# Turning rows by quarters of the PE array in two expert stages, and recurrent scores by halves of 64 keys

## The chip, the cores and the metric

One core of one Trainium2 chip runs the whole program. The time is that of the device in microseconds, from the first to the last instruction and what lies around them; the median of three executions is compared. A core has five engines with a queue of instructions each: TensorE (PE; its weight loads are listed as PEld), VectorE (DVE), ScalarE (ACT), GpSimd (POOL) and SyncE (SP, which here only starts transfers). Matmuls write to PSUM, and DVE or ACT copy the result to SBUF. A matmul has a stationary operand, whose columns are loaded into the array first, and a moving operand, which streams through.

## The reference

Two transformer blocks on 1024 tokens of width 1024, all in float32. The first has a recurrent branch, attention and a mixture of 32 experts, two per token. The second has a gated linear recurrence (HGRN2) beside a pooling branch and a mixture of 64 experts, eight per token. What the change touches:

```python
def block_ffn(args):                  # for each block of tokens of one expert
    xb, e = args
    return (jax.nn.silu(xb @ w_gate[e]) * (xb @ w_up[e])) @ w_down[e]
...
def step(state, inp):                 # HGRN2, per head, chunk by chunk
    ...
    decay = jnp.where(causal, jnp.exp(jnp.minimum(diff, 0.0)), 0.0)
    scores = jnp.einsum('bhtk,bhsk,bhtsk->bhts', qb, kb, decay)
    o_intra = jnp.einsum('bhts,bhsv->bhtv', scores, vb)
```

## The kernel before

The program runs stage after stage, each a set of instruction queues written by hand, one per engine, joined by semaphores. PE executes its queue in order.

**Experts** (`experts`, called once with 32 and once with 64 experts). A step works on two half blocks of 64 tokens, which may belong to two experts. Half A uses columns 0 to 63 of the array and the expert's weights `w_gu`/`w_dn`; half B uses columns 64 to 127 and a staged copy (`st_gu`, `st_dn`, in the tiles `h` or `second`). PE's order in step i is: eight pairs of gate/up matmuls into `gu_ps` (L1870 and L1873, 512 columns each, one pair per chunk of 128 of the 1024 inputs); the turns of the next step's token rows (`turn_rows`, L1859: eight transposes of 128x128 into `x_ps`); the down matmuls of step i-1 into `y_ps` (L1896, L1899, in `finish`); the turns of this step's activation (L1882, two transposes into `h_ps`). Token rows arrive in `moe_xb` by an indirect gather that POOL starts one step and more ahead. DVE copies `x_ps` to `x_t` (L1947) and `h_ps` to `hid_t` (L1949), multiplies the activation (L1945), and stages half B's weights (L1940, L1933). Before the down matmuls PE's sequencer reads the block's expert number from memory (L1887) and works out addresses (L1896); L1857, 1740 and 1864 do the like elsewhere.

**Recurrence** (`hgrn`, four heads). For each tile t of 128 tokens, `scores` (L2120) forms eight 128x128 products, one per level of a halving of the tile and one for the diagonal, into one half of the PSUM tile `big`. DVE multiplies all 8x128 columns by `mask` (L2274) and adds them up over the levels (L2287) into `sc`. PE then multiplies `sc` by the values (L2154) and the carried state by the queries (L2157). Between the scores of tile t+1 and these products PE runs a part of the next head's projection (L2101), except in the last head.

Of the kernel before, what the change touches and what calls it, by code (L numbers as in the profile page):

```python
# [21 lines left out]
ALU = mybir.AluOpType  # L22
ACT = mybir.ActivationFunctionType
AX = mybir.AxisListType.X

P = 128
S = 1024
D = 1024
T = S // P
C = D // P  # L30
BANK = 512
# [13 lines left out]
PART = P // 2  # L45
# [1650 lines left out]


def experts(nc, G, E, NB, W, rows_d, sum_d, loaded, stage, work):

# [3 lines left out]
    ph = phase(nc)  # L1703
    FC = F_EXP // P
    with ph.ctx:
# [5 lines left out]
        xb, idx, mark = G.xb, G.idx, G.mark  # L1711
        act_g = ph.sb("act_g", [P, 2, F_EXP])
        hid = ph.sb("hid", [P, 2, F_EXP])
        hid_t = ph.sb("hid_t", [P, 2, FC, P])
# [6 lines left out]
        y = work[:, 4 * D:6 * D].rearrange("p (s n) -> p s n", s=2)  # L1721
        x_ps = ph.ps("x_ps", [P, C, P])
        gu_ps = ph.ps("gu_ps", [P, 2, 2, F_EXP])
        h_ps = ph.ps("h_ps", [P, BANK // P, P])[:, 0:FC, :]
        y_ps = ph.ps("y_ps", [P, D])
# [129 lines left out]
        def _(pe):  # L1855
            def turn_rows(b, slot, landed):
                pe.wait_ge(x_in[slot], landed)  # L1857
                for c in range(C):
                    last = nc.tensor.transpose(x_ps[:, c, :], xb[:, slot, c:D:C], G.ident[:])  # L1859
                last.then_inc(x_turned, 1)  # L1860

            def step(i, slot, rounds):
# [18 lines left out]
                for c in range(FC):  # L1881
                    last = nc.tensor.transpose(h_ps[:, c, :], hid[:, slot, c::FC], G.ident[:])  # L1882
                last.then_inc(h_turned, 1)
# [41 lines left out]
        def _(v):  # L1925
            d = nc.vector
# [16 lines left out]
            def step(i, slot, rounds):  # L1943
                v.wait_ge(silu_done, i + 1)
                d.tensor_tensor(hid[:, slot, :], act_g[:, slot, :], gu_ps[:, slot, 1, :], ALU.mult).then_inc(hid_ready, 1)  # L1945
                v.wait_ge(x_turned, i + 2)
                d.tensor_copy(x_t[:, 1 - slot], x_ps[:]).then_inc(x_ready, 1)  # L1947
                v.wait_ge(h_turned, i + 1)
                d.tensor_copy(hid_t[:, slot], h_ps).then_inc(h_ready, 1)  # L1949
                v.wait_ge(share_in, i + 1)  # L1950
                d.tensor_copy(share[PART:P, slot:slot + 1], share_b[PART:P, slot:slot + 1]).then_inc(share_ready, 1)
                stage_down(i)
                stage_gate_up(i + 2, slot)

            stage_gate_up(0, 0)
            v.wait_ge(x_turned, 1)
            d.tensor_copy(x_t[:, 0], x_ps[:]).then_inc(x_ready, 1)  # L1957
            stage_gate_up(1, 1)
# [22 lines left out]
def hgrn(nc, A, G):  # L1981
# [8 lines left out]
    ph = phase(nc)  # L1990
# [11 lines left out]
    with ph.ctx:  # L2002
# [17 lines left out]
        kd_t = ph.sb("kd_t", [P, T, P])  # L2020
        sm = ph.sb("sm", [P, N, P])
        sc = ph.sb("sc", [P, 2, P])
# [7 lines left out]
         sc_ps, sc_taken, sc_ready, kt_ready, kt_taken, o_ready, o_taken, u_ready, st_ready, root_in,  # L2030
         rooted, o_done, turned, turn_taken, lb_ready) = ph.sems(
            "w0 w1 w2 w3 gain_in masked proj proj_taken dve act to_exp exped kd_ready lev_ready "
            "sc_ps sc_taken sc_ready kt_ready kt_taken o_ready o_taken u_ready st_ready root_in "
            "rooted o_done turned turn_taken lb_ready")
        w_in_sem = [w0, w1, w2, w3]
# [45 lines left out]
        def _(pe):  # L2081
# [30 lines left out]
            def scores(h, t):  # L2112
                cs = slice(t * P, (t + 1) * P)
                if t == 0:
                    pe.wait_ge(proj_taken, 1 + h * 4 + 4)
                else:
                    pe.wait_ge(sc_taken, h * T + t)
                for lev in range(N):
                    kk, qq = (qk[:, lev, cs], qk[:, lev, cs]) if lev < LEVELS else (k[:, cs], q[:, cs])
                    last = nc.tensor.matmul(big[:, 1, lev * P:(lev + 1) * P], kk, qq, start=True, stop=True)  # L2120
                last.then_inc(sc_ps, 1)

            def head(h, more):
# [24 lines left out]
                for t in range(T):  # L2148
                    if t + 1 < T:
                        scores(h, t + 1)  # L2150
                        if more:
                            project(h + 1, 0, [t + 1])
                    pe.wait_ge(sc_ready, h * T + (t + 1))
                    last = nc.tensor.matmul(ko_ps[:, t, :], sc[:, t % 2, :], val[:, t, :], start=True, stop=t == 0)  # L2154
# [58 lines left out]
        def _(v):  # L2213
# [8 lines left out]
            v.wait_ge(lb_ready, 2)  # L2222
            v.wait_ge(masked, MASKED)
            v.wait_ge(gain_in, 16)

# [5 lines left out]
            with v.Fori(0, H) as h:  # L2231
# [38 lines left out]
                for t in range(T):  # L2270
                    v.wait_ge(sc_ps, h * T + (t + 1))
                    if t:
                        v.wait_ge(sc_ready, h * T + t)
                    d.tensor_tensor(sm[:].rearrange("p n t -> p (n t)"), big[:, 1],  # L2274
                                    mask[:].rearrange("p n t -> p (n t)"), ALU.mult).then_inc(sc_taken, 1)
                    if t == 0:
# [7 lines left out]
                    v.wait_ge(sc_taken, h * T + (t + 1))  # L2284
                    if t >= 2:
                        v.wait_ge(o_ready, h * T + (t - 1))
                    d.tensor_reduce(sc[:, t % 2, :], sm[:].rearrange("p n t -> p t n"), AX, ALU.add).then_inc(sc_ready, 1)  # L2287

# [488 lines left out]
```

## Time and profile before

| | |
|---|---|
| three executions | 3523.74, 3524.87, 3526.46 us, median 3524.87 |
| profiled execution | 3527.6 us, its span 3525.9 us |
| mean granted PE clock | 0.952 of 2.4 GHz |
| PE busy | 91% of the span |
| DVE, ACT, POOL busy | 45%, 21%, 20% |
| DMA | 564.82 MB, mean 160 GB/s |

The trace records each instruction with its start. The ends of matmuls are modelled, so differences between starts are what counts. A plain float32 matmul appears as two records with a weight load each, a transpose as one. The end of a wait is put down to what released it; "issue" means that the engine waited for nothing that the profile shows.

### The profile page before, as it was taken

Reading aid. Unit: us, or ns where it says so; the run is one execution under the profiler, and the core shown is the slowest. Engines: PE = TensorE matmul, PEld = TensorE weight load, DVE = VectorE, ACT = ScalarE, POOL = GpSimd, SP = SyncE. Lnnn points to the kernel's source line nnn. Section 1 sums busy time; section 2 is a strip of 40 time slices with the busy share of each in tenths; the row PEclk is TensorE's granted clock in tenths of the full one; section 3 lists DMA queues with packets and bytes.
Section 4 is the critical chain, followed back from the end, with each engine's and each line's share of the span. In section 5 each row is a group of like instructions: output and inputs, shape, how many; then the busy total and the mean of one; then the engine's idle time right before and its main releaser. Section 6 shows DMA issues by size and latency. Waiting matters only on the chain. (4 is left out here: it accounts for less than half of the span.)

```text
span 3525.9 us, 44548 instructions
## 1 busy us (share of the span) xinstructions
PE 3216.6 (91%) x14147; PEld 1603.9 (45%) x14148; DVE 1579.0 (45%) x2360; ACT 728.2 (21%) x1169; POOL 714.7 (20%) x919
## 2 busy tenths in 40 slices
PE   8999999978999995989789997989899999999992
PEld 4444445545665454333267773455333333333330
DVE  3322224456774123434347773334444444444444
ACT  2221223334552001111023330121011111111112
POOL 1000000000000000344400000000355555555552
PEclk9999999998999996999889998989999999999996
DMA  6210021123221215899531001211788998988876
GB/s 225 96 42 30 0 102 53 49 62 79 73 72 60 73 66 217 316 386 383 181 129 36 24 1 75 75 76 56 270 276 274 351 327 297 309 282 280 272 248 185
DMA packets 177205, 564.82 MB, mean 160 GB/s; under 512 B 18636, under 2 KB 88880, under 8 KB 139952
## 3 DMA queue, kind: packets, MB, share of 16 engines
q1 hardware_dynamic: 139456, 428.64, 32.1%
q0 software_dynamic: 34416, 128.50, 14.9%
q10 hardware_dynamic: 3240, 6.45, 0.5%
q8 instruction: 58, 0.95, 0.1%
q14 instruction: 35, 0.29, 0.0%
HBM read 460.27 MB, written 103.27 MB: 160 GB/s over the span
## 5 line engine op out<-in xcount | busy, mean ns | idle before, releaser
L1870 PE MATMUL gu_ps<-w_gu,second 128*64 x1680 | 754.8, 603 | 12.9 <-DVE second L1957 7.8
L1873 PE MATMUL gu_ps<-h,second 128*64 128x512 f32 x1680 | 754.8, 603 | 0.0
L1870 PEld LDWEIGHTS gu_ps<-w_gu,second 128*64 128x64 f32 x1680 | 224.2, 138 | 455.2 <-issue 443.3
L1503 POOL COPY moe_idx<-moe_slot_tok 128x1 int32<-128x1 int32 x4 | 0.6, 185 | 1878.1 <-DVEq L1438 1236.5
L1896 PE MATMUL y_ps<-w_dn,hid_t 128*64 x824 | 375.6, 598 | 0.2
L1899 PE MATMUL y_ps<-second,hid_t 128*64 128x512 f32 x824 | 375.6, 598 | 0.0
L355 PE MATMUL front<-second,wcol 128*128 128x512 f32 x768 | 332.1, 595 | 4.9 <-ACTq L63 2.5
L1933 DVE COPY h<-w_gu 128x4096 f32 x109 | 249.4, 2288 | 93.4 <-SPq L1751 88.4
L355 PEld LDWEIGHTS front<-second,wcol 128*128 128x128 f32 x768 | 146.3, 191 | 189.8 <-issue 189.8
L1819 POOL TENSOR_TENSOR idx_y<-moe_slot_tok,moe_side 128x1 int32<-128x1 int32 x103 | 122.7, 1191 | 522.5 <-ACT second L1919 522.5
L1873 PEld LDWEIGHTS gu_ps<-h,second 128*64 128x64 f32 x1680 | 224.1, 138 | 0.0
L1919 ACT ACTIVATE second<-y_ps,share 128x1024 f32<-128x1024 f32 x103 | 114.7, 1114 | 456.4 <-PE y_ps L1899 456.4
L1913 ACT ACTIVATE act_g<-gu_ps 128x256 f32<-128x256 f32 x105 | 40.3, 384 | 734.3 <-PE gu_ps L1873 734.3
L1896 PEld LDWEIGHTS y_ps<-w_dn,hid_t 128*64 128x64 f32 x824 | 104.3, 136 | 189.2 <-issue 177.3
L1823 POOL TENSOR_TENSOR mark_y<-tok 128x1 f32<-128x1 f32 x103 | 180.2, 1750 | 20.6 <-DMA token_sums<-second,idx_y 9.9
L1824 POOL DMA_INDIRECT token_sums<-second,idx_y x103 | 176.0, 1708 | 18.3 <-issue 17.4
L1945 DVE TENSOR_TENSOR hid<-act_g,gu_ps 128x256 f32<-128x256 f32 x105 | 44.1, 420 | 291.1 <-ACT act_g L1913 291.0
L1949 DVE COPY hid_t<-h_ps 128x256 f32<-128x256 f32 x105 | 44.5, 424 | 275.8 <-PE h_ps L1882 275.8
L1859 PEld LDWEIGHTS x_ps<-ident,moe_xb 128*128 128x128 f32 x856 | 104.4, 193 | 105.0 <-issue 94.3
L1940 DVE COPY second<-w_dn 128x2048 f32 x105 | 128.9, 1228 | 47.2 <-issue 46.2
L1859 PE MATMUL x_ps<-ident,moe_xb 128*128 128x128 f32 x856 | 125.1, 290 | 18.7 <-PEq L95 17.9
L1947 DVE COPY second<-x_ps 128x1024 f32<-128x1024 f32 x105 | 128.5, 1224 | 24.3 <-PE x_ps L1859 24.3
(449 smaller groups left out, 4904.6 us busy)
## 6 DMA issues: line engine op xcount, KB each, us to landing
w_gu<-in_w_gate_dram SPq DMA_DIRECT2D x96, 1024.0 KB, 12.8
w_gu<-in_w_up_dram SPq DMA_DIRECT2D x96, 1024.0 KB, 15.8
w_dn<-in_w_down_dram SPq DMA_DIRECT2D x96, 1024.0 KB, 10.7
wcol<-in_w_in_dram SPq DMA_DIRECT2D x12, 1024.0 KB, 5.4
qk_by_head<-stage SPq DMA_DIRECT2D x32, 384.0 KB, 3.7
qk<-qk_by_head SPq DMA_DIRECT2D x16, 768.0 KB
token_sums<-zero POOLq DMA_DIRECT2D x19, 512.0 KB, 12.9
token_sums<-second SPq DMA_DIRECT2D x16, 512.0 KB, 2.6
```

The lines of the kernel that those rows point to most:

```text
L355: last = nc.tensor.matmul(ps[:, slot, c, h * BANK:(h + 1) * BANK], wcol[:, k, kc, c * P:(c + 1) * P], G.u[:, kc, h * BANK:(h + 1) * BANK], ...
L1819: g.tensor_tensor(idx_y[:, slot:slot + 1], G.slot_tok[:, bass.ds(b, 1)], G.side, ALU.add).then_inc(idx_y_ready, 1)
L1823: g.tensor_tensor(mark_y[:, slot:slot + 1], G.tok[:, 0:1], G.tok[:, 0:1], ALU.add).then_inc(idx_y_ready, 1)
L1824: g.indirect_dma_start(sum_d, bass.IndirectOffsetOnAxis(ap=idx_y[:, slot:slot + 1], axis=0), y[:, slot, :], None, compute_op=ALU.add).then ...
L1859: last = nc.tensor.transpose(x_ps[:, c, :], xb[:, slot, c:D:C], G.ident[:])
L1870: nc.tensor.matmul(gu_ps[0:PART, slot], x_t[:, slot, c, 0:PART], w_gu[:, bass.ds(ws, 1), :, c, :].rearrange("p o g n -> p (o g) n"), start ...
L1873: last = nc.tensor.matmul(gu_ps[PART:P, slot], x_t[:, slot, c, PART:P], st_gu[:, slot, :, c, :], start=c == 0, stop=c == C - 1)
L1896: nc.tensor.matmul(y_ps[0:PART, cs], hid_t[:, slot, c, 0:PART], w_dn[:, bass.ds(ws, 1), c, cs].rearrange("p o n -> p (o n)"), start=c == 0 ...
L1899: last = nc.tensor.matmul(y_ps[PART:P, cs], hid_t[:, slot, c, PART:P], st_dn[:, c, cs], start=c == 0, stop=c == FC - 1)
L1933: d.tensor_copy(st_gu[:, slot].rearrange("p g c n -> p (g c n)"), w_gu[:, bass.ds(e % W, 1)].rearrange("p o g c n -> p (o g c n)")).then_i ...
L1940: d.tensor_copy(st_dn.rearrange("p c n -> p (c n)"), w_dn[:, bass.ds(e % W, 1)].rearrange("p o c n -> p (o c n)")).then_inc(d_staged, 1)
L1947: d.tensor_copy(x_t[:, 1 - slot], x_ps[:]).then_inc(x_ready, 1)
```

## The change

The transposes of the experts are replaced by plain matmuls with the identity. For the first chunk (`whole`) the full 128x128 block is loaded twice, and 64 columns of the identity are streamed each time. Each further chunk is cut into four quarters of 64x64, each on its own tile of the array, with row half a of the source going to PSUM bank a. `x_ps` and `h_ps` are laid out as two banks for this, and the copies read them in the matching order. In the recurrence the tile of scores is formed only where it is needed: seven products (six levels and the diagonal) for keys and queries of the same half, on two column halves, and one 64x64 product for the widest level. They go to alternate halves of `big[:, 1]`, so `scores` of tile 1 no longer waits for the mask of tile 0. DVE copies the wide piece, masks 448 instead of 1024 columns, and reduces in two instructions of 64 partitions.

```diff
+def turn_quarters(nc, G, out, src, whole):
+    for a in range(2):
+        rows = slice(a * PART, (a + 1) * PART)
+        if whole:
+            last = nc.tensor.matmul(out[:, a, :], src, G.ident[:, rows], start=True, stop=True)
+            continue
+        for b in range(2):
+            cols = slice(b * PART, (b + 1) * PART)
+            last = nc.tensor.matmul(out[cols, a, :], src[rows, cols], G.ident[rows, rows], start=True, stop=True)
+    return last
...
-        x_ps = ph.ps("x_ps", [P, C, P])
+        x_ps = ph.ps("x_ps", [P, 2, C, PART])
-        h_ps = ph.ps("h_ps", [P, BANK // P, P])[:, 0:FC, :]
+        h_ps = ph.ps("h_ps", [P, 2, BANK])[:, :, 0:FC * PART].rearrange("p a (c n) -> p a c n", c=FC)
...
-                    last = nc.tensor.transpose(x_ps[:, c, :], xb[:, slot, c:D:C], G.ident[:])
+                    last = turn_quarters(nc, G, x_ps[:, :, c, :], xb[:, slot, c:D:C], c == 0)
...
-                    last = nc.tensor.transpose(h_ps[:, c, :], hid[:, slot, c::FC], G.ident[:])
+                    last = turn_quarters(nc, G, h_ps[:, :, c, :], hid[:, slot, c::FC], c == 0)
...
-                d.tensor_copy(x_t[:, 1 - slot], x_ps[:]).then_inc(x_ready, 1)
+                d.tensor_copy(x_t[:, 1 - slot].rearrange("p c (a n) -> p a c n", a=2), x_ps[:]).then_inc(x_ready, 1)
...
-        sm = ph.sb("sm", [P, N, P])
+        mask_h = ph.sb("mask_h", [P, LEVELS, PART])
+        sm = ph.sb("sm", [P, LEVELS, PART])
...
-                if t == 0:
+                if t < 2:
                     pe.wait_ge(proj_taken, 1 + h * 4 + 4)
                 else:
-                    pe.wait_ge(sc_taken, h * T + t)
-                for lev in range(N):
+                    pe.wait_ge(sc_taken, h * T + (t - 1))
+                to = t % 2 * BANK
+                for n, lev in enumerate([*range(LEVELS - 1), LEVELS]):
                     kk, qq = (qk[:, lev, cs], qk[:, lev, cs]) if lev < LEVELS else (k[:, cs], q[:, cs])
-                    last = nc.tensor.matmul(big[:, 1, lev * P:(lev + 1) * P], kk, qq, start=True, stop=True)
-                last.then_inc(sc_ps, 1)
+                    for half in range(2):
+                        hs = slice(half * PART, (half + 1) * PART)
+                        nc.tensor.matmul(big[hs, 1, to + n * PART:to + (n + 1) * PART], kk[:, hs], qq[:, hs],
+                                         start=True, stop=True)
+                wide = qk[:, LEVELS - 1, cs]
+                nc.tensor.matmul(big[0:PART, 1, to + LEVELS * PART:to + N * PART], wide[:, 0:PART], wide[:, PART:P],
+                                 start=True, stop=True).then_inc(sc_ps, 1)
...
+                    pe.wait_ge(wide_taken, h * T + (t + 1))
+                    pe.wait_ge(low_ready, h * T + (t + 1))
                     pe.wait_ge(sc_ready, h * T + (t + 1))
...
+            hv = Steps(v, halved)
+            for half in range(2):
+                hs = slice(half * PART, (half + 1) * PART)
+                hv(d.tensor_copy(mask_h[hs, 0:LEVELS - 1], mask[hs, 0:LEVELS - 1, hs]))
+                hv(d.tensor_copy(mask_h[hs, LEVELS - 1], mask[hs, LEVELS, hs]))
+            hv(d.memset(sc[PART:P, :, 0:PART], 0.0))
...
-                    d.tensor_tensor(sm[:].rearrange("p n t -> p (n t)"), big[:, 1],
-                                    mask[:].rearrange("p n t -> p (n t)"), ALU.mult).then_inc(sc_taken, 1)
+                    d.tensor_copy(sc[0:PART, t % 2, PART:P], big[0:PART, 1, to + LEVELS * PART:to + N * PART]
+                                  ).then_inc(wide_taken, 1)
+                    d.tensor_tensor(sm[:].rearrange("p n t -> p (n t)"), big[:, 1, to:to + LEVELS * PART],
+                                    mask_h[:].rearrange("p n t -> p (n t)"), ALU.mult).then_inc(sc_taken, 1)
...
-                    d.tensor_reduce(sc[:, t % 2, :], sm[:].rearrange("p n t -> p t n"), AX, ALU.add).then_inc(sc_ready, 1)
+                    d.tensor_reduce(sc[0:PART, t % 2, 0:PART], sm[0:PART].rearrange("p n t -> p t n"), AX,
+                                    ALU.add).then_inc(low_ready, 1)
+                    d.tensor_reduce(sc[PART:P, t % 2, PART:P], sm[PART:P].rearrange("p n t -> p t n"), AX,
+                                    ALU.add).then_inc(sc_ready, 1)
```

In PE's queue of an expert step, from the last gate/up matmul to the first down matmuls, there stood before (each name is output<-inputs, and the last numbers are partitions x columns of the output):

```order
L1873 MATMUL gu_ps<-h,second 64x512
L1859 MATMUL x_ps<-ident,moe_xb 128x128 x8
L1887 TENSOR_LOAD moe_blk_e
L1887 ISA x2
L1888 REGISTER_ALU
L1896 ISA
L1896 MATMUL y_ps<-w_dn,hid_t 64x512
L1899 MATMUL y_ps<-second,hid_t 64x512
```

and in the changed kernel at the same place (TENSOR_LOAD and what follows it is the sequencer's preparation of the down matmuls):

```order
L1886 MATMUL gu_ps<-h,second 64x512
L1703 MATMUL x_ps<-ident,moe_xb 128x64 x2
L1707 MATMUL x_ps<-ident,moe_xb 64x64 x28
L1900 TENSOR_LOAD moe_blk_e
L1900 ISA x2
L1901 REGISTER_ALU
L1909 ISA
L1909 MATMUL y_ps<-w_dn,hid_t 64x512
```

Thirty matmuls stand where eight transposes stood; nothing else has moved. In PE's queue of the recurrent stage, a head's second and third scores stood before as

```order
L2120 MATMUL big<-qk 128x128 x7
L2120 MATMUL big<-q,k 128x128
L2101 MATMUL big<-h,w 128x512 x2
L2154 MATMUL ko_ps<-val,sc 128x128
L2117 REGISTER_ALU
L2120 MATMUL big<-qk 128x128 x7
```

and in the changed kernel, around the same projection part (L2101 before, L2115 now), as

```order
L2139 MATMUL big<-qk 64x64 x12
L2139 MATMUL big<-q,k 64x64 x2
L2142 MATMUL big<-qk 64x64
L2115 MATMUL big<-h,w 128x512 x2
L2175 ISA
L2178 MATMUL ko_ps<-val,sc 128x128
L2139 MATMUL big<-qk 64x64 x12
```

Eight matmuls of a tile have become fifteen of a quarter of the area each, in the same place of the queue.

## Rows read from the trace of the kernel before

**Rows 1.** Windows: length, busy PE, PEld, DVE, ACT, POOL, clock, DMA share, GB/s.

```profile
1411.52:1744.15 332.63, 310.12 (x1434) 115.23 (x1434) 138.96 (x147) 35.41 (x49) 141.81 (x190) 0.96 0.91 332
...
2491.41:3461.09 969.68, 968.12 (x4624) 363.16 (x4624) 449.67 (x477) 117.72 (x159) 517.40 (x627) 1.00 0.86 287
```

**Rows 2.** The same two expert stages, instructions on tile act_g alone (one activation a step).

```profile
1411.52:1744.15 332.63, 10.47 (x25) 9.61 (x25) 0.96 0.91 332
2491.41:3461.09 969.68, 33.67 (x80) 30.72 (x80) 1.00 0.86 287
```

**Rows 3.** Timeline of PE in one expert step: start, us, engine, line, operands.

```profile
3007.10 0.59 PE L1870 MATMUL gu_ps<-w_gu,second 128*64 x1
...
3007.63 1.15 PE L1859 MATMUL x_ps<-ident,moe_xb 128*128 128x128 f32 x8
3008.71 0.64 PE L1896 MATMUL y_ps<-w_dn,hid_t 128*64 x1
```

**Rows 4.** The same timeline, end of that step and start of the next.

```profile
3011.76 0.59 PE L1896 MATMUL y_ps<-w_dn,hid_t 128*64 x1
...
3012.30 0.50 PE L1882 MATMUL h_ps<-ident,hid 128*128 128x128 f32 x2
3012.73 0.64 PE L1870 MATMUL gu_ps<-w_gu,second 128*64 x1
```

**Rows 5.** Groups by line and shape: records, busy us, mean ns, idle before.

```profile
L1870 PE MATMUL gu_ps<-w_gu,second 128*64 x1680 | 754.8, 603 | 12.9 <-DVE second L1957 7.8 <-DVE second L1947 5.1
...
L1859 PE MATMUL x_ps<-ident,moe_xb 128*128 128x128 f32 x856 | 125.1, 290 | 18.7 <-PEq L95 17.9 <-DMA moe_xb<-token_rows,moe_idx 0.8
...
L2106 PE MATMUL big<-w,h 128*128 128x128 f32 x1024 | 115.0, 275 | 0.0
...
L1945 DVE TENSOR_TENSOR hid<-act_g,gu_ps 128x256 f32<-128x256 f32 x105 | 44.1, 420 | 291.1 <-ACT act_g L1913 291.0
```

**Rows 6.** Timeline of PE in the router's matmuls.

```profile
1289.86 1.87 PE L1162 MATMUL ps<-w_route,h 128*128 128x36 f32 x16
```

**Rows 7.** Timeline of PE and its weight loads (PEld) in one gate/up group.

```profile
3000.61 0.13 PEld L1870 LDWEIGHTS gu_ps<-w_gu,second 128*64 128x64 f32 x1
...
3000.61 0.13 PEld L1873 LDWEIGHTS gu_ps<-h,second 128*64 128x64 f32 x1
...
3000.66 0.14 PEld L1870 LDWEIGHTS gu_ps<-w_gu,second 128*64 128x64 f32 x1
...
3003.23 0.59 PE L1870 MATMUL gu_ps<-w_gu,second 128*64 x1
```

**Rows 8.** Timeline of a step whose token rows landed late.

```profile
2898.39 1.16 PE L1859 MATMUL x_ps<-ident,moe_xb 128*128 128x128 f32 x8 [0.28 <-DMA moe_xb<-token_rows,moe_idx]
...
2899.63 0.64 PE L1896 MATMUL y_ps<-w_dn,hid_t 128*64 x1
```

**Rows 9.** Line 1887 in that step; PEldq is PE's sequencer; first and last start.

```profile
L1887 PEldq FUSED_REGOPS  x2: 42/96/151, 2898.4 to 2898.9; - x2
```

**Rows 10.** Line 1857 in the step of rows 7.

```profile
L1857 PEldq FUSED_REGOPS  x1: 42/42/42, 3003.3 to 3003.3; - x1
```

**Rows 11.** Timeline of PE in the recurrent stage, one tile of a head.

```profile
2028.15 0.39 PE L2157 MATMUL ko_ps<-state,qb 128*128 128x128 f32 x2
2028.37 1.73 PE L2120 MATMUL big<-qk 128*128 128x128 f32 x14
...
2030.16 1.88 PE L2101 MATMUL big<-h,w 128*128 128x512 f32 x4
...
2032.10 0.28 PE L2157 MATMUL ko_ps<-state,qb 128*128 128x128 f32 x1
```

**Rows 12.** Timeline of DVE in the last head of that stage.

```profile
2104.73 1.94 DVE L2287 TENSOR_REDUCE sc<-sm 128x128 f32<-128x1024 f32 x1
2106.84 1.22 DVE L2274 TENSOR_TENSOR sm<-big,mask 128x1024 f32<-128x1024 f32 x1 [0.17 <-PE big L2120]
2108.09 1.93 DVE L2287 TENSOR_REDUCE sc<-sm 128x128 f32<-128x1024 f32 x1
```

More of the change, by code:

```diff
@@ L1946, in step @@
                 v.wait_ge(x_turned, i + 2)
-                d.tensor_copy(x_t[:, 1 - slot], x_ps[:]).then_inc(x_ready, 1)
+                d.tensor_copy(x_t[:, 1 - slot].rearrange("p c (a n) -> p a c n", a=2), x_ps[:]).then_inc(x_ready, 1)
                 v.wait_ge(h_turned, i + 1)
-                d.tensor_copy(hid_t[:, slot], h_ps).then_inc(h_ready, 1)
+                d.tensor_copy(hid_t[:, slot].rearrange("p c (a n) -> p a c n", a=2), h_ps).then_inc(h_ready, 1)
                 v.wait_ge(share_in, i + 1)
@@ L1956, in _ @@
             v.wait_ge(x_turned, 1)
-            d.tensor_copy(x_t[:, 0], x_ps[:]).then_inc(x_ready, 1)
+            d.tensor_copy(x_t[:, 0].rearrange("p c (a n) -> p a c n", a=2), x_ps[:]).then_inc(x_ready, 1)
             stage_gate_up(1, 1)
@@ L2030, in hgrn @@
          sc_ps, sc_taken, sc_ready, kt_ready, kt_taken, o_ready, o_taken, u_ready, st_ready, root_in,
-         rooted, o_done, turned, turn_taken, lb_ready) = ph.sems(
+         rooted, o_done, turned, turn_taken, lb_ready, wide_taken, low_ready, halved) = ph.sems(
             "w0 w1 w2 w3 gain_in masked proj proj_taken dve act to_exp exped kd_ready lev_ready "
             "sc_ps sc_taken sc_ready kt_ready kt_taken o_ready o_taken u_ready st_ready root_in "
-            "rooted o_done turned turn_taken lb_ready")
+            "rooted o_done turned turn_taken lb_ready wide_taken low_ready halved")
         w_in_sem = [w0, w1, w2, w3]
@@ L2223, in _ @@
             v.wait_ge(masked, MASKED)
+            hv = Steps(v, halved)
[4 more added lines that the diff above has]
+            hv(d.memset(sc[PART:P, :, 0:PART], 0.0))
+            hv.join()
             v.wait_ge(gain_in, 16)
@@ L2273, in _ @@
                         v.wait_ge(sc_ready, h * T + t)
-                    d.tensor_tensor(sm[:].rearrange("p n t -> p (n t)"), big[:, 1],
-                                    mask[:].rearrange("p n t -> p (n t)"), ALU.mult).then_inc(sc_taken, 1)
+                    if t >= 2:
+                        v.wait_ge(o_ready, h * T + (t - 1))
+                    to = t % 2 * BANK
+                    d.tensor_copy(sc[0:PART, t % 2, PART:P], big[0:PART, 1, to + LEVELS * PART:to + N * PART]
+                                  ).then_inc(wide_taken, 1)
+                    d.tensor_tensor(sm[:].rearrange("p n t -> p (n t)"), big[:, 1, to:to + LEVELS * PART],
+                                    mask_h[:].rearrange("p n t -> p (n t)"), ALU.mult).then_inc(sc_taken, 1)
                     if t == 0:
@@ L2284, in _ @@
                     v.wait_ge(sc_taken, h * T + (t + 1))
-                    if t >= 2:
-                        v.wait_ge(o_ready, h * T + (t - 1))
-                    d.tensor_reduce(sc[:, t % 2, :], sm[:].rearrange("p n t -> p t n"), AX, ALU.add).then_inc(sc_ready, 1)
+                    d.tensor_reduce(sc[0:PART, t % 2, 0:PART], sm[0:PART].rearrange("p n t -> p t n"), AX,
+                                    ALU.add).then_inc(low_ready, 1)
+                    d.tensor_reduce(sc[PART:P, t % 2, PART:P], sm[PART:P].rearrange("p n t -> p t n"), AX,
+                                    ALU.add).then_inc(sc_ready, 1)
                 v.wait_ge(proj_taken, 1 + h * 4 + 4)
```

## The prediction

> **What bounds the kernel now.** I read the page first: TensorE is busy for 91% of the span (in the table above). Such a share says little alone, so next come the windows of the stages that the change touches [rows 1, 2]. The reader is to see two things there. The second expert stage is 969.68 us long with PE busy for 968.12 us at a granted clock of 1.00, that is 2.4 GHz, and ran 80 steps (80 activations of act_g): 12.12 us a step. The first ran 25 steps in 332.63 us; at 12.13 us a step these are 303.3 us, so 29 us of it are waits for weights that had not landed (DMA share 0.91).
>
> Then the timeline of one expert step, PE alone [rows 3, 4]. Everything in it follows without a gap: the last gate/up pair starts at 3007.10, the eight turns of the rows (L1859) at 3007.63, the first down pair at 3008.71, the last at 3011.76, the two turns of the activation (L1882) at 3012.30, the next gate/up pair at 3012.73. So whatever the turns get longer or shorter by, the step gets longer or shorter by. A gate/up pair takes 0.43 us (3000.61 to 3003.23 are six of them, the first 0.48 [rows 7]).
>
> **What a turn costs now.** Eight turns span 1.15 us with the last record's own 0.275, so the last one starts 0.88 us after the first: 0.21 to the second, then 0.11 each [rows 3, 5]; the second is 0.1 late because its load, too, had to wait for the new shape. The two neighbours work on column halves (128*64), the turns on the whole array (128*128), and each change of shape shows: the last gate/up pair to the first turn is 0.53, 0.10 more than a pair; the last turn to the down pair 1.08 - 0.88 = 0.20, of which 0.11 is the turn; and the first pair after a change is 0.48 instead of 0.43, as the load of 64 columns is not hidden then. A change costs about 0.10 us plus a bare load: 0.05 for 64 columns, 0.10 for 128. The 0.11 of a turn is its load, not its columns: the router's matmuls, only 36 columns wide, start as far apart (sixteen records in 1.87 - 0.28 us, fifteen steps of 0.106), and those of L2106, 128 columns, take 115.0/1024 = 0.112 [rows 5, 6]. The load of 64 columns must then be about 0.055, and the two column halves load side by side (L1870 and L1873 both at 3000.61, the next of L1870 at 3000.66) [rows 7].
>
> **What replaces it.** A turn is one record (856 for 107 blocks); a plain f32 matmul is two (L1870: 8 matmuls a step, 1680 records in 105 steps), each with its own load [rows 5]. Per block of rows the change puts 2 whole matmuls (4 records, 128 columns loaded) and 28 quarter ones (56 records) for 8. A quarter record loads 64 columns, 0.055, beside the one before it, and streams 64 columns; 512 take 0.43, so 64 take 0.054. If the four tiles run side by side as the two column halves do, a group of four records takes 0.056: 14 groups. From the first start: whole records at 0, 0.21, 0.32 and 0.44; change of shape, first group at 0.64; second at 0.75 (bare load); last at 0.75 + 12 x 0.056 = 1.42; down pair at 1.42 + 0.15 = 1.57. Against 1.08 that is +0.49 us. For the activation: 0.44 + 0.20 = 0.64, second group 0.75, next gate/up pair 0.90, against 0.43: +0.47. The quarters cannot win even so, since the seven quartered chunks stream 7 x 2 x 0.056 = 0.78 where seven turns took 0.77, and two more changes of shape and the doubled first chunk come on top.
>
> **Who issues them.** The sequencer works in order. After the turns it fetches the block's expert for the down matmuls (L1887 on), and how long that takes is seen where rows came late: turns start at 2898.39, L1887 begins at 2898.4 (all eight turns were then issued), the down pair starts at 2899.63 [rows 8, 9]. So 1.2 us from the last turn issued to the down pair, now hidden because the issue runs ahead. How far ahead: L1857, behind all gate/up matmuls, runs at 3003.3, when the seventh of sixteen pairs has just started: 18 matmul records outstanding [rows 7, 10]. With sixteen records of turns they all fit. With 60 the last is issued when 18 are left, 4.5 groups or 0.25 us before the last start: at 1.17. Then 1.2 us: down pair at 2.37 against 1.08. **+1.29 us instead of +0.49.** Behind the activation's turns (12 records) the same kind of preparation for gate/up has the 3.5 us of down matmuls as cover; if that cover were gone it would cost up to 0.5 us more. The next gather of rows is issued off a longer step, so it is not late.
>
> The Trainium skill (TensorE: Matmul & The Clock Gate, first table) gives the TensorE queue as 64 instructions deep. Rows 7 and 10 show 18 matmul records, 34 with their loads. By a depth of 64 the preparation would begin 0.2 us earlier, the step would grow by 1.56, and the sum would be some 20 us lower.
>
> So a step grows by 1.29 + 0.47 = 1.76 us. Second stage: 80 x 1.76 = +141. First stage: 25 x 1.76 = 44, less what the 29 us of waiting for weights take up; the waits come in three places and the loads themselves wait for freed slots, so I take about 20 as absorbed: +24 (bounds +15 and +44). The first blocks' turns: +1. The copies out of PSUM keep their elements, and DVE is busy for less than half of this stage [rows 1]. The larger program is left at nothing: PE's other instructions do not change.
>
> **Recurrent scores.** Per tile of 128 tokens PE now runs sixteen records of 0.112 from 2028.37, then four of the next projection from 2030.16, and with two small products comes round in 3.95 us (2028.15 to 2032.10 for the second product) [rows 11]. After: 28 records in pairs on two column halves, 14 x 0.056, two more for the wide piece, 0.11, and two changes of shape. From the product's last start to the projection's second: 0.20 + 0.11 + 12 x 0.056 + 0.11 + 0.15 + 0.54 = 1.78, against 17 x 0.112 + 0.43 = 2.33: -0.55 us. Three heads x 8: -13. The second scores of each head no longer wait for the first mask: -0.6 x 3. In the last head there is no projection and DVE sets the pace: 2104.73 to 2108.09, 3.36 us for a reduction of 1.94 and a mask of 1.22 [rows 12]. After: copy 0.22 (estimate from 0.42 for 256 elements [rows 5]), mask 448/1024 elements 0.62, two reductions of 0.85 to 0.92 each (half the partitions, 448 elements): about 2.75, -0.6 x 8 = -5. In the other heads 2.75 stays below PE's new 3.4, so that cover holds; if it did not, the gain would end at 3.95 - 2.75 = 1.2. Copies that build mask_h fall before the first head's activation and are left at nothing; without cover, +2. Sum -20 (bounds -12 and -28).
>
> **Sum:** 141 + 24 + 1 - 20 = +146 on the profiled execution's 3527.6 us, 3673.6. That execution is 2.7 above the median 3524.87, so 3671.
>
> **Rivals.**
> The four tiles do not load or start side by side in full: no row of this kernel shows row halves. If the two row halves load one after another, a group takes 0.11: the last starts at 0.64 + 0.165 + 12 x 0.11 = 2.13, issued 0.5 earlier, down pair at 2.83, +1.75; activation +0.53. Step +2.28: 182 + 37 + 1 - 20 = 200, 3725. Chance 0.20. The Trainium skill (the same page, "Wait — 56ns, not 53.3ns?") says that starts of matmuls never come closer than about 25 ns on average however small they are. By it a group of four would take 0.1 and the time would be near 3713. Two loads start together in rows 7, but no row has four matmuls within 0.056 us, so the trace neither bears it out nor excludes it.
>
> The records of one matmul and the next stay in order and do not overlap across tiles: 0.056 a record, the last start at 0.75 + 54 x 0.056 = 3.77, issued 1.0 earlier, down pair at 3.97, +2.9; activation +0.8. 80 x 3.7 + 92 - 20 + 1 - 20 = 349: 3874. Against it: column halves pair in every step [rows 7]. 0.12.
>
> The preparation stays hidden (a deeper queue, or records of quarters that count for less): step +0.96, 77 + 10 (of 24, the rest absorbed) + 1 - 20: 3593. Against it: rows 7 and 10. 0.12.
>
> PE's clock falls to 1.2 GHz in part of the step, since it now idles for 0.8 us: a tenth of the step at half speed is +1.2 us, +126 on top: about 3800. Against it: the clock is still 0.96 in the first stage with its 29 us of waits [rows 1]. 0.04.
>
> Faster: the changes of shape are free when the matmuls around them are tiled too, and a quarter record costs 0.03. Then the turns take 0.45 + 14 x 0.03 = 0.87 for 1.08 and 0.45 + 2 x 0.03 = 0.51 for 0.43, and two bare loads of 0.05 go: about 0.2 us off each step: 105 x 0.2 + 20 gives 3484. It decides where a step grows by less than 20/105 = 0.19 us. Against it: a change between 128*64 and 128*128 costs in each step [rows 3, 4]. 0.05, no change at all 0.02. What is left, 0.45, is my forecast, alone from 3640 to 3710.
>
> **Range.** From 3585 (the hidden preparation) to 3790 (row halves that load in turn, nothing absorbed in the first stage, +20, and the cover of the gate/up preparation gone, 80 x 0.5 = +40): 0.77 and a little of the clock's case. This kernel's runs lie within 0.1%, so 0.2% (7 us) is about what can be told from no change. Slower 0.93, within 0.02, faster 0.05.
>
> **What would show it.** Periods of the gate/up pairs near 13.9 us in the second stage; 60 records per block in the turns, groups of four starts 0.056 apart; PE idle of about 0.8 us before each down pair, put down to issue; fewer weight waits in the first stage; recurrent stage 20 us shorter with scores of 1.2 us. Wrong would be: groups at 0.1 or more, no idle before the down pair, or a step below 12.3 us.

## The result and the profile after

The changed kernel takes 3776.09 us (median, 3771.84 to 3778.22) against 3525.27 for the kernel before (3523.74 to 3526.46) beside it: 7.2% longer, ratio 1.0715, 95% interval 1.0698 to 1.0732. The forecast was 3671 with a range of 3585 to 3790. So the sign and the range held, but the loss is 251 us where 146 were forecast. Its profiled span is 3770.2 us, 244 above the 3525.9 of before.

The windows of the two expert stages (columns as in [rows 1]):

```profile
1409.84:1785.80 375.96, 366.92 (x2984) 172.59 (x2984) 139.64 (x147) 35.77 (x49) 125.60 (x190) 0.98 0.84 294
2508.67:3707.70 1199.03, 1171.43 (x9584) 551.74 (x9584) 449.75 (x477) 118.10 (x159) 408.35 (x627) 0.99 0.74 232
```

Against [rows 1] the first stage grew by 43.3 us (forecast 24) and the second by 229.4 (forecast 141). What lies outside the two got 28 us shorter (244.3 - 272.7), where 19 were forecast. So the surplus over the forecast sits in the expert steps. This is PE's timeline of one step, to be laid beside [rows 3, 4]:

```profile
3024.53 0.59 PE L1883 MATMUL gu_ps<-w_gu,second 128*64 x1
...
3025.05 1.16 PE L1703 MATMUL x_ps<-ident,moe_xb 128*128 128x64 f32 x4
3026.15 1.91 PE L1707 MATMUL x_ps<-ident,moe_xb 64*64 64x64 f32 x56
3028.39 0.64 PE L1909 MATMUL y_ps<-w_dn,hid_t 128*64 x1 [0.33 <-issue]
...
3031.97 0.68 PE L1703 MATMUL h_ps<-ident,hid 128*128 128x64 f32 x4
3032.58 0.35 PE L1707 MATMUL h_ps<-ident,hid 64*64 64x64 f32 x8
3032.86 0.64 PE L1883 MATMUL gu_ps<-w_gu,second 128*64 x1
```

Read it in differences of starts. From the first turn to the first down pair it is 3.34 us, where it was 1.08 and 2.37 were forecast. From the activation's turns to the next gate/up pair it is 0.89, where it was 0.43 and 0.90 were forecast. The step is 14.84 us instead of 12.12 (forecast 13.88). So all of the surplus, 0.96 us, lies between the first turn of the token rows and the first down pair. Two parts of that stretch are longer than forecast: four whole records take 1.10 us to the first quarter (forecast 0.64), and the fourteen groups of four take 1.91 - 0.285 (the last record's own) = 1.63 us (forecast 0.78). Part of this is given back ahead of the down pair (below). The groups by form of the loads (PEld), and of the down matmuls, say more:

```profile
L1707 PEld LDWEIGHTS x_ps<-ident,moe_xb 64*64 64x64 f32 x5992 | 190.0, 212 | 7.3
L1703 PEld LDWEIGHTS x_ps<-ident,moe_xb 128*128 128x128 f32 x428 | 109.7, 329 | 103.8 <-issue 103.8
L1703 PEld LDWEIGHTS h_ps<-ident,hid 128*128 128x128 f32 x420 | 57.5, 196 | 83.7 <-issue 83.6
L1707 PEld LDWEIGHTS h_ps<-ident,hid 64*64 64x64 f32 x840 | 22.4, 134 | 7.1
```

```profile
L1909 PE MATMUL y_ps<-w_dn,hid_t 128*64 x824 | 392.1, 621 | 35.2 <-issue 35.2
```

The same helper loads the same shapes for `x_ps` in 329 and 212 ns and for `h_ps` in 196 and 134. What differs is the source: `moe_xb` is read with a step of 8 elements (`c:D:C`), `hid` with a step of 2 (`c::FC`). And there is the idle time ahead of the down matmuls put down to issue that was forecast, 0.33 us in the step above (forecast some 0.8). Line 1900, which reads the expert's number, ran in that step at (PEldq is PE's sequencer; last numbers are first and last start)

```profile
L1900 PEldq FUSED_REGOPS  x2: 42/96/151, 3027.2 to 3027.6; - x2
```

that is 0.6 us before the last turn starts (3026.15 + 1.63 = 3027.78) and 1.2 us before the down pair.

**Ten long steps.** Ten of the 105 steps take 16.55 us instead of 14.84. Windows of one ordinary step and of the long one behind it:

```profile
3602.07:3616.91 14.84, 14.50 (x126) 6.87 (x121) 5.65 (x6) 1.50 (x3) 5.17 (x8) 1.00 0.88 282
3616.91:3633.44 16.53, 16.20 (x126) 7.28 (x121) 5.65 (x6) 1.50 (x3) 5.23 (x8) 0.90 0.52 143
```

and PE's timeline inside the second:

```profile
3627.26 0.91 PE L1909 MATMUL y_ps<-w_dn,hid_t 128*64 x1 [0.33 <-issue]
...
3628.82 1.06 PE L1909 MATMUL y_ps<-w_dn,hid_t 128*64 x1
...
3629.67 1.06 PE L1909 MATMUL y_ps<-w_dn,hid_t 128*64 x1
```

The down pairs behind the turns stand 0.85 us apart instead of 0.43: twice as long, the lower level of 1.2 GHz, and the granted clock of the step is 0.90 for 1.00. That costs 10 x 1.7 = 17 us in all. The hit steps do not lie at random: the seven of the second stage start at 2627.0, 2777.2, 2927.3, 3122.0, 3272.1, 3466.8 and 3616.9, that is 10 or 13 steps apart (150.1 to 150.2 or 194.7 us), and nothing in between.

**The recurrent stage.** PE's timeline of one tile (beside [rows 11]) and DVE's in the last head (beside [rows 12]):

```profile
2064.93 0.39 PE L2181 MATMUL ko_ps<-state,qb 128*128 128x128 f32 x2
2065.25 0.92 PE L2139 MATMUL big<-qk 128*64 128x64 f32 x24
...
2066.33 1.98 PE L2115 MATMUL big<-h,w 128*128 128x512 f32 x4
...
2068.37 0.39 PE L2181 MATMUL ko_ps<-state,qb 128*128 128x128 f32 x2
```

```profile
2121.81 0.22 DVE L2308 COPY sc<-big 64x64 f32<-64x64 f32 x1
2122.05 0.62 DVE L2310 TENSOR_TENSOR sm<-big,mask_h 128x448 f32<-128x448 f32 x1
2122.71 0.93 DVE L2321 TENSOR_REDUCE sc<-sm 64x64 f32<-64x448 f32 x1
2123.67 0.91 DVE L2323 TENSOR_REDUCE sc<-sm 64x64 f32<-64x448 f32 x1
2124.68 0.22 DVE L2308 COPY sc<-big 64x64 f32<-64x64 f32 x1
```

A tile comes round in 3.44 us where it was 3.95 (forecast 3.40), and in the last head DVE's cycle is 2.87 where it was 3.36 (forecast 2.75). From the first product with the state (L2157, now L2181) to the last the stage takes 240.15 us where it took 259.59.

### The profile page after: what moved, and what is told of

Read it like the earlier page. It is cut to its first block and busy times, and to the rows that moved or that the text cites. A ratio compares the mean times of both kernels' runs of the same rounds, so it can differ in the third digit from the quotient of the medians.

```text
span 3770.2 us, 58750 instructions
## 1 busy us (share of the span) xinstructions
PE 3454.8 (92%) x21209; PEld 1825.2 (48%) x21210; DVE 1566.1 (42%) x2429; ACT 727.8 (19%) x1169; POOL 586.4 (16%) x919
## 3 DMA queue, kind: packets, MB, share of 16 engines
q8 instruction: 66, 1.08, 0.1%
## 5 line engine op out<-in xcount | busy, mean ns | idle before, releaser
L1909 PE MATMUL y_ps<-w_dn,hid_t 128*64 x824 | 392.1, 621 | 35.2 <-issue 35.2
L1912 PE MATMUL y_ps<-second,hid_t 128*64 128x512 f32 x824 | 392.6, 621 | 0.0
L1837 POOL DMA_INDIRECT token_sums<-second,idx_y x103 | 324.1, 3146 | 45.7 <-issue 45.6
L1707 PE MATMUL x_ps<-ident,moe_xb 64*64 64x64 f32 x5992 | 204.8, 285 | 0.0
L1707 PEld LDWEIGHTS x_ps<-ident,moe_xb 64*64 64x64 f32 x5992 | 190.0, 212 | 7.3
L1832 POOL TENSOR_TENSOR idx_y<-moe_slot_tok,moe_side 128x1 int32<-128x1 int32 x103 | 19.1, 186 | 894.5 <-ACT second L1932 894.5
```

What stands on the lines that cost most here:

```text
L1707: last = nc.tensor.matmul(out[cols, a, :], src[rows, cols], G.ident[rows, rows], start=True, stop=True)
L1837: g.indirect_dma_start(sum_d, bass.IndirectOffsetOnAxis(ap=idx_y[:, slot:slot + 1], axis=0), y[:, slot, :], None, compute_op=ALU.add).then ...
L1909: nc.tensor.matmul(y_ps[0:PART, cs], hid_t[:, slot, c, 0:PART], w_dn[:, bass.ds(ws, 1), c, cs].rearrange("p o n -> p (o n)"), start=c == 0 ...
L1912: last = nc.tensor.matmul(y_ps[PART:P, cs], hid_t[:, slot, c, PART:P], st_dn[:, c, cs], start=c == 0, stop=c == FC - 1)
```

## Experiments

Theories of the surplus: (A) a plain float32 matmul loads a source whose elements lie 32 bytes apart in twice the time, and the four tiles do run side by side; (B) the tiles of the two row halves load in turn (a rival of the prediction); (C) two starts cannot come closer than some floor, whatever is loaded. And of the wait before the down pair: the sequencer's preparation is exposed, or it is not. The kernels below that turn other elements of the rows route the second block's tokens otherwise and run a step or two more, so steps are compared, not only totals. A kernel for which no interval is given was executed once, and its steps are read from that profile.

**The two parts apart.** `scores_only` has the experts of before and the recurrent stage of the change; `experts_only` the other way round.

> The experts as before (eight transposes a step), the recurrent scores as changed. Theory A, the two parts of the change are independent and the recurrent stage alone gained its 22 us: 3525.3 - 22 = 3503 us (ratio 0.9938), both expert stages as long as before (332.6 and 969.7 us within 1). Rival, the gain of the recurrent stage is given back behind it, where weights or rows wait on something else: 3518 or more. What would show it is the sum of the expert stages being some 15 us longer.

> The recurrent scores as before, the experts as changed. If the parts are independent: 3776 + 22 = 3798 us, expert steps of 14.84 us in the second stage as in the changed kernel, and again about ten steps of 105 that are 1.7 us longer with down matmuls at a lower clock. Rival: the longer steps depend on the rest of the program, and they are fewer or at other places: 3780.

Measured: `scores_only` 3506.09 us, ratio 0.9938 (0.9916 to 0.9961). Its windows of the experts, 24 steps and 78 steps from start to start,

```profile
1408.70:1729.02 320.32, 298.36 (x1376) 110.77 (x1376) 133.31 (x141) 33.92 (x47) 137.06 (x182) 0.95 0.93 342
2469.67:3415.96 946.29, 944.96 (x4508) 354.44 (x4509) 438.52 (x465) 114.80 (x155) 494.52 (x611) 1.00 0.88 291
```

are as long as before (320.50 and 945.52 for the same steps), so nothing is given back. `experts_only` took 3800.21 us; its usual step is 14.84 us, and eleven are about 1.7 us longer (forecast some ten), at other places. The parts are independent: 3506 + 3800 - 3527 (before, beside them) = 3779 for the 3776 of the changed kernel.

**Neighbouring elements.** `unit_stride` is the changed kernel with

```diff
-  last = turn_quarters(nc, G, x_ps[:, :, c, :], xb[:, slot, c:D:C], c == 0)
+  last = turn_quarters(nc, G, x_ps[:, :, c, :], xb[:, slot, c * P:(c + 1) * P], c == 0)
```

> The changed kernel with one edit: the turns of the token rows read 128 neighbouring elements of a row instead of every eighth one, so the chunks hold other inputs than the weights expect; the instructions, their number and their tiles stay. Theory A, the load of a source with a step of 8 elements (32 bytes) takes twice as long as that of a source without, and the four tiles load side by side: whole records 0.112 us apart instead of 0.237, groups of four 0.056 instead of 0.120, last turn 1.4 us after the first instead of 2.74, and the wait for the preparation shows in full (1.17 + 1.2 = 2.4 us from the first turn to the first down pair, where it was 3.35): step 14.84 - 0.95 = 13.9 us, the whole 3776 - 105 x 0.95 = 3676 us. Rival B, the tiles of the two row halves load in turn, whatever the source: groups stay 0.12 apart and only the first four whole records come closer, by 0.4 us in all: step 14.4 us, 3734. Rival C, a floor of starts: groups at 0.10, step about 14.5.

Measured: 3693.12 us with 107 steps instead of 105, most of them 13.91 us long, and none with its down matmuls at the lower clock. PE's timeline, the load group by form, and line 1900:

```profile
2979.33 0.66 PE L1703 MATMUL x_ps<-ident,moe_xb 128*128 128x64 f32 x4
2979.92 1.04 PE L1707 MATMUL x_ps<-ident,moe_xb 64*64 64x64 f32 x56
...
2981.74 0.64 PE L1909 MATMUL y_ps<-w_dn,hid_t 128*64 x1 [0.78 <-issue]
```

```profile
L1707 PEld LDWEIGHTS x_ps<-ident,moe_xb 64*64 64x64 f32 x6104 | 101.2, 136 | 8.5 <-issue 0.8
```

```profile
L1900 PEldq FUSED_REGOPS  x2: 42/96/151, 2980.5 to 2981.0; - x2
```

The load fell from 212 to 136 ns, the quarters span 1.04 - 0.22 (own) = 0.82 us for 14 groups, the last turn starts 1.41 us after the first and the down pair at 2.41. These are the prediction's 1.42 and 2.37, though two misses of about 0.05 us cancel in the first: the quarters begin at 0.59 (forecast 0.64) and span 0.82 (forecast 0.78). Rival B (groups of 0.12) and rival C (0.10) are out. The preparation begins 0.21 us before the last turn starts, with 16 records of turns still to start (forecast 0.25 and 18), and the wait put down to issue is 0.78, as forecast; in the changed kernel itself the slower turns covered 0.60 us of the preparation.

**How the price depends on the step.** `stride4` reads every fourth element (`xb[:, slot, c * PART:c * PART + BANK:4]`), `stride2` every second.

> The changed kernel with the turns of the token rows reading every fourth element (16 bytes) instead of every eighth (32 bytes), other inputs again. It tells how the load grows with the step: if it doubles only beyond 16 bytes, groups of four are 0.056 apart and the step is 13.9 us as with neighbouring elements; if it grows evenly, 1.5 times (0.085, step about 14.2); if any step costs double, 0.120 and 14.84. The activation's turns, whose step is 2 elements, went at 0.118 for 128 columns, which speaks against the last. I take 13.9, 3680 to 3695 us.

> The changed kernel with the turns of the token rows reading every second element (8 bytes), other inputs again. A step of 16 bytes cost as much as one of 32, and the activation's turns, with a step of 8 bytes, loaded in 0.118 us for 128 columns. If that low price belongs to the step: whole records 0.118 apart, groups of four 0.06, last turn 1.45 us after the first, step 13.9, whole 3695 us (with the two more blocks of the other unit-order kernels). If instead anything but neighbours costs double and the activation was spared for another reason (its tile, its few records): groups 0.120 and step 14.84, 3795.

The groups by form of the loads, first `stride4`, then `stride2`:

```profile
L1707 PEld LDWEIGHTS x_ps<-ident,moe_xb 64*64 64x64 f32 x6104 | 192.9, 211 | 7.5
```

```profile
L1707 PEld LDWEIGHTS x_ps<-ident,moe_xb 64*64 64x64 f32 x6048 | 103.2, 137 | 8.2 <-issue 0.7
```

`stride4` took 3795.74 us with steps of 14.81 us, and my 13.9 for it was wrong: 16 bytes cost all that 32 cost. `stride2` took 3678.43 us with steps of 13.96, 0.05 above those of neighbours. Over the four steps tried (1, 2, 4 and 8 elements) the price is a jump between 8 and 16 bytes, not a slope; a step of three was not run. The Trainium skill (SBUF — State Buffer, under Door 1: The DMA port swizzle) has SBUF read in lines of 16 bytes, at full speed only where at least two accesses fall on one line. Two float32 elements that lie 8 bytes apart can share such a line and two that lie 16 apart cannot, and the trace agrees (137 ns at two, 211 at four); the page's own figure of four float32 for free is not what these runs show. I had not looked at it for the prediction. The rule would have warned that these loads cost more; how much more it does not say.

**A plain whole matmul, and a transpose.** `plain_whole` is the kernel before with its eight transposes written as plain matmuls, and `transpose_unit` the kernel before with transposes of neighbours:

```diff
-  last = nc.tensor.transpose(x_ps[:, c, :], xb[:, slot, c:D:C], G.ident[:])
+  last = nc.tensor.matmul(x_ps[:, c, :], xb[:, slot, c:D:C], G.ident[:], start=True, stop=True)
```

> The kernel before, its eight transposes of the token rows written as eight plain 128x128 matmuls with the identity (16 records, whole array, same source with a step of 8 elements); nothing is in quarters. Theory A, a plain float32 matmul loads a source of that step in 0.237 us for 128 columns: sixteen records span 15 x 0.237 + 0.05 = 3.6 us from first to last, the preparation behind them is hidden (16 records fit in what runs ahead), so the first down pair stands 3.9 us after the first turn, a step is 12.12 + 2.8 = 14.9 us, the whole some 3525 + 105 x 2.8 = 3820 us less a little weight waiting. Rival B, the slow loads belong to quarters and to what mixes with them: 15 x 0.112 + 0.1 = 1.8 us, step 13.0, whole 3620.

> The kernel before with its eight transposes reading 128 neighbouring elements of a row, so the chunks hold other inputs than the weights expect. Theory A, a transpose (one record) isn't slowed by the step of its source, as its 0.11 us was already that of loads without a step: turns 0.11 apart as before, step 12.12, whole 3525 us but for a block or two more or fewer of the second routing. Rival B, transposes pay for the step too and would go at 0.056: step 12.12 - 0.4 = 11.7, whole 3483 us.

Timeline of PE and the load group of `plain_whole`:

```profile
3048.59 4.07 PE L1859 MATMUL x_ps<-ident,moe_xb 128*128 128x128 f32 x16
3052.59 0.64 PE L1896 MATMUL y_ps<-w_dn,hid_t 128*64 x1
```

```profile
L1859 PEld LDWEIGHTS x_ps<-ident,moe_xb 128*128 128x128 f32 x1712 | 415.4, 334 | 103.8 <-issue 103.8
```

It took 3799.51 us (forecast some 3820) with steps of 15.04: sixteen records span 4.07 - 0.41 = 3.66 us, 0.24 each, with no quarter in the program. So the slow load belongs to plain float32 matmuls of that source (theory A, 3.6 and 14.9 forecast). For `transpose_unit`, timeline and load group:

```profile
2906.00 1.09 PE L1859 MATMUL x_ps<-ident,moe_xb 128*128 128x128 f32 x8
2907.02 0.64 PE L1896 MATMUL y_ps<-w_dn,hid_t 128*64 x1
```

```profile
L1859 PEld LDWEIGHTS x_ps<-ident,moe_xb 128*128 128x128 f32 x872 | 94.4, 142 | 106.5 <-issue 97.3 <-DMA moe_xb<-token_rows,moe_idx 9.2
```

It took 3544.30 us with two steps more; the step is 12.06 us instead of 12.12, and the turn to the down pair 1.02 instead of 1.08. Beside it the load group of the kernel before, and the last seven of its eight turns, then the last seven of `transpose_unit`:

```profile
L1859 PEld LDWEIGHTS x_ps<-ident,moe_xb 128*128 128x128 f32 x856 | 104.4, 193 | 105.0 <-issue 94.3 <-DMA moe_xb<-token_rows,moe_idx 10.7
```

```profile
3007.84 0.94 PE L1859 MATMUL x_ps<-ident,moe_xb 128*128 128x128 f32 x7
```

```profile
2906.17 0.93 PE L1859 MATMUL x_ps<-ident,moe_xb 128*128 128x128 f32 x7
```

A transpose of neighbours loads in 142 ns, and with the step of 8 in 193. So a transpose does pay for the step, about 50 ns of load, but only 0.06 us of it come out in a whole step: neither theory had that. Nearly all of it is the second turn's, which starts 0.17 us after the first instead of 0.21. The other turns stand 0.11 apart in both kernels ((0.94 - 0.27)/6 and (0.93 - 0.27)/6), so their pace does not follow the length of their load.

**The preparation.** `number_first` is the changed kernel with the read of the expert's number (`value_load`) taken from `finish` and put ahead of the turns of the token rows; `both` adds the source of `unit_stride`.

> The changed kernel with one instruction group moved: the sequencer reads the expert's number for the down matmuls before the turns of the token rows are issued, not after; the addresses are still worked out after them. Theory A, the preparation behind the turns is exposed: of the 1.2 us from its start to the first down pair the read of the number is the greater part (0.5 us of waits and register work between the two records of the profile, some 0.8 with the read itself), so the wait of PE before the down pair, 0.4 to 0.6 us now, shrinks to its bare load: step 14.84 - 0.45 = 14.4 us, whole 3776 - 105 x 0.45 = 3729 us (ratio to before 1.058). Rival B, the 0.62 us from the last turn to the down pair is the last quarter group's long load and the change of shape, not the sequencer: step 14.84, 3776 us. Rival C, the read is now exposed in front of the turns, since the queue has run dry there: step longer by up to 0.5, 3820 us.

> The changed kernel with neighbouring elements as the source of the token rows' turns, and the read of the expert's number moved ahead of them. If the first forecast had all its parts right but for the load's length, the turns take 1.42 us to the last and the down pair follows 0.21 behind it if what is left of the preparation is short: step 13.91 - 0.79 = 13.1 us. If the read of the number is only the 0.40 us that its move gave, and the rest still waits, 13.5 us. Whole: 3715 - 105 x 0.9 = 3620 to 3650 us. Even so the step stays about 1.0 us or more above the 12.12 of before.

Timelines of PE, first `number_first`, then `both`:

```profile
2994.36 1.16 PE L1703 MATMUL x_ps<-ident,moe_xb 128*128 128x64 f32 x4
2995.45 1.91 PE L1707 MATMUL x_ps<-ident,moe_xb 64*64 64x64 f32 x56
2997.30 0.64 PE L1910 MATMUL y_ps<-w_dn,hid_t 128*64 x1
```

```profile
2926.57 0.66 PE L1703 MATMUL x_ps<-ident,moe_xb 128*128 128x64 f32 x4
2927.15 1.04 PE L1707 MATMUL x_ps<-ident,moe_xb 64*64 64x64 f32 x56
2928.23 0.64 PE L1910 MATMUL y_ps<-w_dn,hid_t 128*64 x1
```

`number_first` took 3715.98 us, ratio to before 1.0535 (1.051 to 1.056), 60 us less than the changed kernel. The turns are as long as they were, and the down pair now follows the last turn at 0.21 us (2997.30 - 2997.08) with no idle time: step 14.43. That is 105 x 0.40 = 42 us; the rest is that no step has slow down matmuls any more, 10 x 1.7 = 17. Both rivals are out: had the wait not been the preparation's, the step would have stayed at 14.84, and had the read come onto the path in front of the turns, it would have grown. `both` has steps of 13.17 us (3616.25 us in all): the down pair stands 1.66 after the first turn instead of 2.41, so the read was 0.75 of the 1.2 us of preparation. What is left, 13.17 - 12.12 = 1.05 us a step, is the cost of turning by plain matmuls with next to no wait (0.04 us) and no slow load in it; the prediction's bare sum for it was 0.96.

**The activation alone.** `h_only` is `scores_only` with the activation's turns of the change.

> The kernel before with the changed recurrent scores and, in the experts, only the activation's two transposes as two whole and four quarter matmuls; the token rows keep their eight transposes. Forecast by the term of the prediction: 0.90 us from the first turn to the next gate/up pair instead of 0.43, step 12.12 + 0.47 = 12.59, the preparation of the gate/up matmuls hidden by the down matmuls: 3503 + 105 x 0.47 less some weight waiting = 3545 us. Rival, the 0.46 seen in the changed kernel depended on the quarters of the token rows nearby (cover or clock): step 12.12 + 0.3 or less, or steps with down matmuls at the lower clock here too.

```profile
2906.42 0.69 PE L1703 MATMUL h_ps<-ident,hid 128*128 128x64 f32 x4
2907.03 0.35 PE L1707 MATMUL h_ps<-ident,hid 64*64 64x64 f32 x8
```

```profile
L1872 PEld LDWEIGHTS x_ps<-ident,moe_xb 128*128 128x128 f32 x856 | 105.2, 195 | 104.9 <-issue 103.9 <-DMA moe_xb<-token_rows,moe_idx 1.0
```

These are the timeline of PE and the load group of its transposes. Steps are 12.59 us, just the 0.47 forecast, and the whole is 3538.26 us, 7 less than forecast: 24 steps of the first stage take 316.52 us where they took 320.50 before, so there the waits for weights took up all of it. In quarters or with its transposes nearby, the activation's part costs the same.

**The version that is faster than both**, `scores_only`, executed again more often:

> The version that kept the recurrent scores of the change and none of its turns, once more with more rounds, since its first interval was 0.45% wide: ratio to before 0.9938 (22 of 3525 us), between 0.992 and 0.995. If part of the 22 us was chance, the ratio lies above 0.996.

It took 3504.89 us, ratio 0.9939 (0.9926 to 0.9952): 21 and 22 us less than before, in two measurements. A version with every chunk of the rows in quarters was not tried.

## Why the forecast came out short

**The step that failed** is in "What replaces it": "A quarter record loads 64 columns, 0.055". I took that price, and 0.11 for a whole record, from gate/up, router and L2106 loads, all of operands other than the one to be turned. For `moe_xb` with its step of 8 elements it measured twice that. The transposes seemed to confirm 0.11 for 128 columns at the same step, but "The 0.11 of a turn is its load, not its columns" is not borne out by them: with loads of 142 ns instead of 193 they still start 0.11 apart (`transpose_unit`). What sets their pace was not tested. That it equals the price of a plain record of neighbours (`unit_stride`, load of 192 ns) was therefore no evidence for the price of a plain record of this source (load of 334 ns, 0.24 apart). A number that agrees with a row of another kind is no confirmation.

What that one term did: whole records +0.46 us and quarters +0.85, less the 0.35 by which longer turns covered more of the preparation, is +0.96 a step. In the second stage 80 x 0.96 = 77 us and seven long steps 12 us: 89, for the 88 by which that stage missed. In the first stage 25 x 0.96 = 24 and 5 for three long steps, less some 10 more of absorbed waiting: 19, for 19. The 10 is what is left over, but the stage bears it out: 25 x 14.84 + 3 x 1.7 is already its whole length (375.96), so all 29 us of waits for weights were absorbed and not 20.

**What was luck.** The forecast alone reached from 3640 to 3710. The range went on to 3790 for the sake of a rival, loads in turn, which `unit_stride` ruled out; 3776 fell into that part for another reason. (Its upper end is not even what its terms give: 3725 + 20 + 40 = 3785.) And some misses cancel: the clock's 17 us, for which the forecast had nothing, are about offset by the waits above, which took up 9 more than assumed, and by the 28 us outside the two stages, 9 more than forecast. These 28 are also 7 more than `scores_only` gained, but its executions alone range from 3495.74 to 3510.28, so nothing is read from it.

**What held.** Four tiles side by side: `unit_stride` gives 0.82 us for 14 groups with the first gap bare, so the rival of loads in turn fell, although the changed kernel's groups of 0.12 us look just like the 0.11 which that rival had forecast; they had another reason. The 1.2 us of preparation, and about the 18 records that run ahead: 1.2 us from line 1900 to the down pair in both kernels, 16 records outstanding, and 2.41 for 2.37. The bare step of the rival with hidden preparation, 12.12 + 0.96 = 13.08, shows up in `both` (13.17), once the read is moved and neighbours are loaded. The changes of shape and bare loads: +0.47 for the activation, twice. The recurrent stage: -21 in `scores_only` for -20; the two cycles above give 24 x 0.51 + 8 x 0.49 = 16 of it, and the timeline has some more at the change of heads: one head comes round in 74.4 us instead of 79.75, 5.4 less, of which its eight tiles give 4.1. So 1.3 a head lies between heads, where the prediction put 0.6 for the first wait; what else shrank there was not followed up.

**The clock.** The rival that it falls was half right: not in each step, but in ten, in the down matmuls behind the turns. What goes before the fall is the stretch from the first turn to the down pair, 3.34 us in which PE runs small quarters and then waits. With 2.94 us of it and no wait (`number_first`) no down matmuls were slow, nor with 2.41, though 0.78 of that is waiting (`unit_stride`), nor with 4.00 us of whole records (`plain_whole`); with the 3.32 of `stride4` they were in six steps. So neither the wait nor the length of the turns does it alone. What decides which steps are hit was not settled; their even distances (106, 150 or 195 us in the changed kernel, 239 or 283 in `stride4`) speak for something that recurs by itself rather than for the data or the weights of a step, but no run tested it.

The Trainium skill (TensorE: Matmul & The Clock Gate, first table) gives a queue of 64; the sequencer got to line 1900 only 0.21 us before the last turn started, with 16 matmul records outstanding (`unit_stride`), so this case again shows less. The same page's floor of 25 ns between starts (Wait — 56ns, not 53.3ns?) would make the 55 gaps between the 56 quarter records at least 1.4 us; in `unit_stride` they took 0.82. On four tiles the floor does not hold.

## What to carry to other kernels

Price a load by the operand that is to be loaded: its step in memory counts as much as its columns, and a transpose's row says nothing about a plain matmul's. Before replacing few records by many in an engine's queue, count what runs ahead of the sequencer; what it prepares next (here a read of 0.75 us) comes onto the path once the work behind is longer than that, and may be moved ahead of it. Where a change has two parts with opposite signs, run each alone: here one is worth 22 us and the other costs 273.

## What was not expected of the hardware

Plain float32 records that load 128 columns start 0.11 to 0.12 us apart at a step of 1 or 2 elements and 0.24 at a step of 4 or 8 (64 columns on four tiles: groups of four 0.06 and 0.12 apart). A transpose starts every 0.11 us at a step of 1 or 8, although its load takes 142 ns at the one and 193 at the other. Quarters on four tiles start 15 ns apart on average (0.82 us for 55 gaps in `unit_stride`). The clock can drop to its lower level behind 3.3 us of turns and a wait, in steps that otherwise keep the higher one, and then costs 1.7 us, here in about one step of ten and at even distances.
